# Differential keys and queries turned by VectorE inside the retention heads

## What is computed

```python
dq = apply_rope(to_diff_heads(dq_), cos_d, sin_d)      # queries, 4 heads x 2 halves x 64
dk = apply_rope(to_diff_heads(dk_), cos_d, sin_d)      # keys of the latent stream
k_all = jnp.concatenate([cdk, dk], axis=3)             # keys of the context stream in front
v_all = jnp.concatenate([cdv, dv], axis=2)

def diff_attend(q, k, v, lam):
    s = jnp.einsum('bhmqd,bhmkd->bhmqk', q, k) * (DIFF_DQK ** -0.5)
    p = jax.nn.softmax(s, axis=-1)
    a = p[:, :, 0] - lam * p[:, :, 1]
    return jnp.einsum('bhqk,bhkv->bhqv', a, v)
```

## Time and profile before

| what | value |
|---|---|
| median of 3 runs | 1789.92 us |
| lowest and highest run | 1789.9 and 1791.22 us |
| span of the profiled execution | 1788.2 us |
| TensorE busy | 1770.3 us (99%) |
| GpSimd busy | 1360.3 us (76%) |
| ScalarE busy | 1035.8 us (58%) |
| VectorE busy | 802.1 us (45%) |

### The profile page before, as it was taken

How to read it: one execution, slowest core, us unless ns; L and a number is a source line. 1 busy time by engine, 2 the same in 40 slices (tenths; PEclk the granted TensorE clock), 3 DMA queues, 4 the chain that set the end, 5 groups by cost and what they waited for, 6 DMA issues and landing times.

```text
span 1788.2 us, 25437 instructions
## 1 busy us (share of the span) xinstructions
PE 1770.3 (99%) x9135; PEld 1479.6 (83%) x9135; DVE 802.1 (45%) x1590; ACT 1035.8 (58%) x1537; POOL 1360.3 (76%) x573
## 2 busy tenths in 40 slices
PE   7999999999999999999999999999999999999998
PEld 4888888888888888888888878898888888888887
DVE  2782344844334546332446974321112985431112
ACT  4645675445676754466655576555555566745554
POOL 5867787866778878666869766778887975688886
PEclk9999999999999999999999999999999999999999
DMA  9975556754456567455547644556655754456663
GB/s 367 315 237 159 172 169 208 235 165 141 143 167 209 167 209 244 133 143 154 191 136 221 181 127 135 177 170 193 188 189 170 207 158 130 142 186 192 188 188 129
DMA packets 171555, 327.88 MB, mean 183 GB/s; under 512 B 10433, under 2 KB 16065, under 8 KB 171457
## 3 DMA queue, kind: packets, MB, share of 16 engines
q1 hardware_dynamic: 168272, 320.22, 57.9%
q10 hardware_dynamic: 3184, 6.32, 1.0%
HBM read 325.46 MB, written 1.05 MB: 183 GB/s over the span
## 4 chain that ended last, share of the span: by engine, by line
PE 69%; POOL 14%; issue 14%; DMA 1%; POOLq 0%; ACT 0%; DVE 0%; SPq 0%; DVEq 0%; ACTq 0%
PE G L1934 16%; PE G L1936 16%; PE G L1935 16%; POOL wlo L528 14%; PE A L2636 3%; PE G L2636 3%; PE A L1934 2%; PE A L1936 2%; PE A L1935 2%; PE A L2637 1%; PE G L2637 1%; PE A L2403 1%; PE G L2425 1%; PE A L1988 1%; DMA raw<-in_w_in 1%
## 5 line engine op out<-in xcount | busy, mean ns | idle before, releaser
L528 POOL TENSOR_TENSOR wlo<-raw,whi 128x1024 fp32r<-128x1024 f32 (+1 forms) x568 | 1356.6, 2399 | 414.4 <-ACT whi L553 411.6
L553 ACT ACTIVATE whi<-raw 128x1024 fp32r<-128x1024 f32 (+1 forms) x568 | 593.4, 1048 | 568.2 <-PE G L1936 438.0
L1934 PE MATMUL G<-whi,hparts 128*128 128x512 f32 (+1 forms) x1472 | 580.0, 394 | 1.0 <-DVE hparts L1290 0.6
L1936 PE MATMUL G<-whi,hparts 128*128 128x512 f32 (+1 forms) x1472 | 567.9, 386 | 0.0
L1935 PE MATMUL G<-wlo,hparts 128*128 128x512 f32 (+1 forms) x1472 | 567.6, 386 | 0.0
L1934 PEld LDWEIGHTS G<-whi,hparts 128*128 128x128 f32 x1472 | 276.4, 188 | 59.7 <-issue 5.8
L1936 PEld LDWEIGHTS G<-whi,hparts 128*128 128x128 f32 x1472 | 276.3, 188 | 56.5
L1935 PEld LDWEIGHTS G<-wlo,hparts 128*128 128x128 f32 x1472 | 276.7, 188 | 51.7
L1685 DVE STREAM_TRANSPOSE t<-z 32x256 f32<-32x256 f32 (+2 forms) x256 | 96.7, 378 | 3.8
L1934 PE MATMUL G<-whi,osplit 128*128 128x512 f32 x240 | 94.2, 393 | 0.0
L1936 PE MATMUL G<-whi,osplit 128*128 128x512 f32 x240 | 93.4, 389 | 0.0
(11 more groups left out here) (432 smaller groups left out, 2509.3 us busy)
## 6 DMA issues: line engine op xcount, KB each, us to landing
raw<-in_w_in SPq DMA_DIRECT2D x324, 512.0 KB, 3.8
raw<-in_w_up SPq DMA_DIRECT2D x64, 512.0 KB, 3.7
raw<-in_w_down SPq DMA_DIRECT2D x64, 512.0 KB, 3.3
raw<-in_w_out SPq DMA_DIRECT2D x40, 512.0 KB, 3.7
raw<-in_w_branch_out SPq DMA_DIRECT2D x36, 512.0 KB, 4.3
modw<-in_w_mod SPq DMA_DIRECT2D x32, 512.0 KB, 5.1
raw<-in_w_branch SPq DMA_DIRECT2D x24, 512.0 KB, 3.3
modz<-in_w_mod SPq DMA_DIRECT2D x16, 512.0 KB, 9.7
```

Of the source, the lines that this page charges most:

```text
L528: pool.tensor_tensor(wlo[:, s, :, 0:n], raw[:, s, :, 0:n], whi[:, s, :, 0:n].bitcast(F32), ALU.subtract)\
L553: act.activation(whi[:, slot, :, 0:n], raw[:, slot, :, 0:n], ACT.Copy).then_inc(hi_ready, 1)
L1934: pe.matmul(bank, hi, whi[:, slot, kk, 0:n], start=first, stop=False)
L1936: return pe.matmul(bank, lo, whi[:, slot, kk, 0:n], start=False, stop=last)
```

## The change

In the latent passes the differential keys and queries are no longer turned by TensorE and copied by ScalarE. `turn_diff_heads(part)` on VectorE turns them from `z` into `tT` in 32 instructions of 32x256 elements, spread over the five iterations of the retention heads as 6, 6, 7, 6 and 7, each time as the iteration's last work. The last of them raises a new semaphore, `diff_heads`, for which TensorE waits before the first differential scores. The 16 transposes of groups 4 to 7 and the four copies go, in each of the two passes. The factor of the queries is applied in the rotation, whose four products become `scalar_tensor_tensor` for all four chunks (factor 1.0 except for the queries).

```diff
@@ ScalarE
-                    evacuate(1, columns(z, DV) if is_x else ctx_values, ACT.Copy, beside=beside_dv)
+                    evacuate(1, columns(z, DV) if is_x else ctx_values, ACT.Copy, beside=None if is_x else beside_dv)
@@ VectorE, rotation
-                            dve.tensor_tensor(s1, x1, sin, ALU.mult)
-                            link(dve.tensor_tensor(s2, x2, sin, ALU.mult))
-                            dve.tensor_tensor(x1, x1, cos, ALU.mult)
-                            link(dve.tensor_tensor(x2, x2, cos, ALU.mult))
+                            factor = DH ** -0.5 if c == 3 else 1.0
+                            dve.scalar_tensor_tensor(s1, x1, factor, sin, ALU.mult, ALU.mult)
+                            link(dve.scalar_tensor_tensor(s2, x2, factor, sin, ALU.mult, ALU.mult))
+                            dve.scalar_tensor_tensor(x1, x1, factor, cos, ALU.mult, ALU.mult)
+                            link(dve.scalar_tensor_tensor(x2, x2, factor, cos, ALU.mult, ALU.mult))
@@ VectorE, retention heads
+                def turn_diff_heads(part):
+
+                    for m in range(32 * part // (H1 + 1), 32 * (part + 1) // (H1 + 1)):
+                        a, col = ((2, DKc), (3, DQ))[m // 16]
+                        rows, feats = (slice(q * PART, (q + 1) * PART) for q in divmod(m % 16, 4))
+                        ins = dve.transpose(tT[feats, a].rearrange("p h (t s) -> p t h s", t=TT)[:, :, :, rows],
+                                            z[rows, :, col:col + W].rearrange("p t (h f) -> p t h f", f=P)[:, :, :, feats])
+                    if part == H1:
+                        ins.then_inc(diff_heads, 1)
...
+                    if is_x:
+                        turn_diff_heads(i)
@@ TensorE
-                    if c == 3:
+                    if c == 3 and not is_x:
                         for g in ((4,), (5,), (6, 7), ())[s]:
                             head_group(g)
...
+                if is_x:
+                    pe.wait_ge(diff_heads, w(diff_heads))
                 for h in range(H1):
                     for t in range(TT):
```

More of the change, by code:

```diff
@@ L351, in build @@
         mlp_vn, mlp_mixed = sem("mlp_vn"), sem("mlp_mixed")
+        diff_heads = sem("diff_heads")
         branches_ready = sem("branches_ready")
```

## The result

| | median, us | runs, us | profiled execution: time, span |
|---|---|---|---|
| before | 1790.07 | 4, from 1789.9 to 1791.22 | 1789.92, 1788.2 |
| changed | 1797.99 | 4, from 1797.21 to 1798.2 | 1797.21, 1795.3 |

The ratio of the changed kernel to the one before is 1.0042, with a 95% interval of 1.0029 to 1.0055: slower by 0.42%, or 7.9 us. The prediction was 1793.7 us with a range of 1791.5 to 1797.5. The direction was right, the loss was about twice the 3.8 us that were forecast, and the median lies 0.5 us above the range.

What follows compares the result with a forecast made beforehand. TensorE was taken to bound both latent passes. Removed transposes (-3.8 us) plus the added wait (+7.6 us), other terms at nothing, gave +3.8 us: 1793.7 us from 1789.92, range 1791.5 to 1797.5.

Steps and rivals of the forecast that it cites:

- The transposes that went: TensorE's DV chunks: 16 transposes fewer a latent pass save 1.9 us (bounds 1.75 and 2.0), 3.8 us in both.
- The copies of ScalarE: Four copies a pass go, beside TensorE's slabs on an engine that waits for TensorE anyway: nothing gained.
- The added wait: TensorE before the first differential scores waits for VectorE's last seven transposes: 3.8 us a pass, 7.6 us in both.
- rival 2: VectorE's last seven transposes take 0.35 us each: wait 3.1 us, net loss 2.4 us, 1792.3 us; chance 15%.
- Transposes inside the heads: The other 25 transposes, within the retention-head iterations, are covered and cost nothing; without cover 2.7 us a head.
- i = 2: Example iteration of the retention heads: six transposes (2.7 us) follow the addition at 395.32, leaving 3.5 us before the cross products.
- The rotation: VectorE's 32 changed products a pass: +0.06 us each, counted as 0, at most 0.4 us in one pass.
- Rival 3: TensorE catches up the 3.8 us in the late slabs from filled buffers, leaving only the gain: 1786.1 us; chance 5%.
- rival 1: TensorE's clock falls in the new pause, 1.8 us a fall: 1795.5 us for one pass, 1797.3 for both; chance 22%.
- bound of 2.6: Most a clock fall would lose: half of a slow stretch of at most 5 us at the span's start.

Runs made afterwards that it cites:

- none last: Changed kernel with its 32 transposes spread 8, 8, 8, 8 and 0, so none stands behind the last addition: 1786.31 us, ratio 0.9976 to the kernel before.
- The series: Changed kernel with 1, 3, 5, 6 or 10 transposes behind the last addition, or a late slab moved there: medians from 1788.5 to 1801.36 us.
- ten last: Changed kernel with ten of its 32 transposes behind the last addition (5, 6, 6, 5 and 10): 1801.36 us, ratio 1.006 to the kernel before.
- three last: Changed kernel with three of its 32 transposes behind the last addition (7, 7, 7, 8 and 3): 1791.95 us, ratio 1.0007 to the kernel before.

## Why the prediction was right in direction and too low

**The transposes that went: right.** Counted 1.9 us a pass, measured 1.86 and 1.87 in the changed kernel; the kernels without turning and without the wait came out 3.9 and 3.8 us below the one before, where the sum had 3.8.

**The copies of ScalarE: right,** in the sense that with all of the change but the wait nothing is missing from the 3.8 us.

**The added wait: right.** Counted 3.8 us, measured 3.76 in each pass. Its steps in VectorE's timeline:

```profile
415.69 0.42 DVE L1604 TENSOR_TENSOR o<-G,e 128x256 f32<-128x256 f32 x1 [1.94 <-PE G L2402]
...
416.15 3.14 DVE L1568 STREAM_TRANSPOSE tT<-z 32x256 f32<-32x256 f32 x7
```

The first transpose began 0.46 us behind the addition's start instead of 0.35, and TensorE's next weight load 0.05 us behind the last transpose instead of 0.12, two errors that nearly cancel. The seven took 3.14 us instead of 3.15, and their group by line has 422, 436 and 442 ns as shortest, median and longest:

```profile
L1568 DVE STREAM_TRANSPOSE tT<-z x64: 422/436/442, 379.6 to 756.5; 32x256 f32<-32x256 f32 x64
```

So rival 2 (cheap transposes) fell. The estimate that the prediction worked out from the Trainium skill, "Vector Engine (DVE) Microarchitecture Reference", section 3.8, was 0.27 us for each; the trace has 0.45 from start to start, and it was right to sum by the row of the same form.

**Transposes inside the heads: right.** The view of waits has no other wait of TensorE for VectorE's line 1568, and the kernel with eight a head lost nothing. The iteration that the prediction calls i = 2 is i = 1 (with i = 2 there are seven); the cover is as it says.

**The rotation: right,** at the lower bound, 0: each product takes what it took. The sums ahead of line 2200 ended in time in the changed kernel, since those eight transposes began at 368.79 with no idle time before them.

**Rival 3 (the wait is given back) fell.** The kernel with matmuls of no use keeps the two waits without a fall, and it is 7.6 us slower than the one with none last (1793.95 against 1786.31): nothing of 2 x 3.76 us came back.

**The clock, which the sum put at nothing, is the step that failed.** The sum adds the transposes that went and the wait, and leaves the clock behind the wait at 0 us. The runs showed +1.70 and +1.71 us there in the profiled execution, so 1786.3 + 7.5 + 3.4 = 1797.2, which is that execution's time (1797.21). This is rival 1, which had the mechanism, the places and the price on record (1797.3 us for two falls) with a chance of 22%. That its price came so near is in part luck: the 1.8 us was taken, not worked out, below a bound of 2.6 from the earlier trace rows.

What was wrong is the sentence "Against it: 3.8 is barely above 3.4, and one fall tells little". The trace had one fall, at the end of the program, and I took its 3.4 us as an edge that the new pause would hardly pass. One observed fall gives a length that sufficed once; it says nothing of shorter ones. The series shows falls at little more than half of it and, by the run times, in all 18 pauses of the changed kernel's nine runs. With 3.76 us above the only length known to bring a fall, and nothing known against it, a fall in both passes should have been the forecast. The Trainium skill ("TensorE: Matmul & The Clock Gate", section "What's actually happening") describes the low clock as the default state from which activity lifts the engine. The rows agree with that in kind: 0.50 behind the pause, and 1.00 again in 423 to 424 with TensorE at work.

**The top of the range is what follows from it.** 1797.5 stood 0.2 us above the time of two falls, as though this case had no width. The first comparison gave 1797.99 us, the second one of the same kernel 1797.07. The kernel before gave 1790.07 and 1790.06 beside them, so the 0.9 us are this kernel's own. The three unprofiled executions of the first comparison, 1797.99 to 1798.2, have a mean granted clock of 0.996 over the span, the profiled one 0.998 and that of the second comparison 0.997. That points to more time at the low clock. The trace of ten last shows two ways to it, a stay of 6.8 us instead of 3.4 and a fall elsewhere in the span; which it was here remains open, since these executions have no traces.

## What to carry to other kernels

When work moves off the engine that sets the time and a wait takes its place, price the wait twice: by its length, and by what the engine's clock does behind it. The second price comes or doesn't, and its odds grow with the pause, so when a new pause is as long as one that once brought a fall, the fall belongs in the forecast and not among its rivals. And the last place before a consumer is the dearest for such work: the same 32 transposes, with eight in each of the earlier heads and none behind the last addition, turned a loss of 7.9 us into a gain of 3.8. (All these pauses lie at one place of one program; what other work around a pause does to the odds is not shown.)

## What the runs showed of the hardware that was not expected

- Behind pauses of equal length the clock falls in one pass and not in the other of the same execution (1.96 and 3.31 us). No fall showed behind 1.06 us in 22 pauses, one in thirteen traces behind the 1.2 us near 40 us of the span, and four or more at every length from 1.84 us on (by run times at 1.84 us, by the granted clock from 1.96 us on).
- The fall need not lie in the pause. With three last it came at about 418.05, some 0.7 us after TensorE had resumed work, and in the second trace of the changed kernel at 420.3, 1.1 us after, so the first matmuls behind the pause run at full speed. The scores then took 2.96 us instead of 3.73, and the slab behind them paid the rest: the pass lost 1.7 us all the same.
- In the changed kernel the clock stayed at its lower level from about 419.3 to 422.7, and half of these 3.4 us is the 1.7 us. With ten last it stayed for 6.8 us in one pass.
- Matmuls of no use in the pause avoid the fall, at no cost where the engine would stand anyway: 1793.95 us against 1797.07 for the changed kernel.
- A product of VectorE in the scalar-and-tensor form from PSUM takes 416 ns at 128x256, as the plain form does.
